# The start of a hybrid attention and mLSTM layer: its conditioned input tiles made in another order, in pairs, with the gate rows in four column groups

## The chip, the cores and the metric

The kernel runs on one core of a Trainium2 chip. The metric is the device time of one execution in microseconds (us), over 3 runs. All data are float32; inputs and outputs lie in the chip's main memory (HBM).

## What is computed

One layer of a decoder: 1024 tokens, width 1024, all parameters float32. Cut to what matters:

```python
shift, scale, gate = jnp.split(jax.nn.silu(c) @ w_ada + b_ada, 3, axis=-1)
h = x * (1.0 + scale[:, None, :]) + shift[:, None, :]
proj = h @ w_in + b_in        # 1024 x 6664: q,k,v,z | q,k,v,o,z,i,f | merge gates
y_sb = stick_breaking_attention(sb_q, sb_k, sb_v)              # 8 heads of 64
y_sb = (y_sb * silu(sb_z)) @ w_sb_proj
mq, mk = split(silu(causal_depthwise_conv(concat(ml_q, ml_k), conv_w, conv_b)))
hm = mlstm_chunkwise(mq, mk, ml_v, ml_i, log_sigmoid(ml_f))     # 4 heads of 128
y_ml = (head_norm(hm) * sigmoid(ml_o) * silu(ml_z)) @ w_ml_proj
y = (sigmoid(g_sb) * y_sb + sigmoid(g_ml) * y_ml) @ w_out
return layer_norm(alpha * x + (1.0 + gate[:, None, :]) * y, ln_g, ln_b)
```

The change concerns the first two lines and the first columns of the third.

## The kernel before

**Tiles.** The input h is kept transposed: 8 tiles `hH[:, d]` and `hL[:, d]` of 128 features by 1024 tokens. Each number is split into a high part in the rounded type fp32r and the rest, so that a product takes three matmuls: high by high, low by high, high by low (`split_product`). After the input tiles come the projection jobs (`project`, 48 matmuls of 512 tokens each), then four iterations of attention and mLSTM with further projection jobs between, the merge and the output product.

**The tile stage.** The change is in the stage that makes the 8 tiles. For each tile d:
- SyncE's queue (`block.sync`) loads 128 columns of x (`x_rows`, 512 KB) and the shift and scale columns of the conditioning weights (`a_raw`, two transfers of 512 KB). Rows of these transfers are 128 numbers, 512 B. `a_raw` has three buffers.
- VectorE (`ada_rows`) multiplies the 8 row blocks of `a_raw` by silu(c) and sums them into two accumulators, then adds these.
- TensorE (`ada_columns`) sums over partitions with a column of ones; VectorE (`mod_columns`) adds the bias and writes the shift and scale of the tile to `mod`.
- TensorE (`turn_x`) transposes x in 8 blocks of 128 x 128; ScalarE (`shifted`) applies scale and shift out of two PSUM banks into `h_raw`, and rounds it into `hH`; VectorE (`low_h`) makes `hL`.
- TensorE (`tile_of`) multiplies the tile by the first three weight chunks (`w_proH`, `w_proL`): n = 0 are the 8 columns of the input and forget gates (rows i and f), n = 1 and 2 are the first q and k. That is 18 matmuls, all with 512 tokens. Sums stay in six PSUM banks over all tiles.

Each engine works through its program in the order in which it is written, with semaphores between engines; nothing is scheduled by a planner. In the code `t.matmul(out, a, b)` holds a (the weights) still and streams b.

**What comes after.** The gate rows are copied with their bias into `r_if` (ScalarE, `bias_copy`), spread by 8 small transfers to `r_f` and `r_i` (`q` runs over four partition groups), and go through logarithms and scans on ScalarE and VectorE (`row_logs`, `row_columns`). TensorE does the jobs 3 and 4 (`project`) meanwhile, and then turns the rows into columns (`gate_columns`). The split of weight chunk 9, which the second half of job 4's columns need, stands behind `row_logs` on VectorE (`pro_split(PRO_CHUNKS + 3)`).

**The small parameters.** Seven transfers (c, the biases, the convolution weights and the norm weights) fill `prm` from SyncE's queue ahead of all else. TensorE turns `prm` into columns (`cols`), from which silu(c) is made.

## Time and profile before

| | us |
|---|---|
| median of 3 runs | 959.51 (959.13 to 959.73) |
| the profiled execution's own time | 959.67 |
| its span, first to last instruction | 957.8 |
| TensorE busy | 928.8 (97%) |
| VectorE busy | 616.0 (64%) |
| ScalarE busy | 441.2 (46%) |

All times are those of one profiled execution. PE is TensorE's matmul side, DVE VectorE, ACT ScalarE, POOL GpSimd, SP SyncE; a q behind a name is its queue, which issues transfers. Busy time of PE counts each matmul to its modelled end, so two neighbours overlap; its pace is read from start to start.

### The profile page before, as it was taken

What the parts mean: (1) busy time and instruction counts of PE and PEld (TensorE: products, weight loads), DVE (VectorE), ACT (ScalarE), POOL (GpSimd) and SP (SyncE); (2) the same over time, 40 slices, a digit from 0 to 9 for tenths busy, and PEclk for the clock granted to TensorE, in tenths of its full rate; (3) what the DMA queues carried; (4) which work ended last, traced back from release to release, by engine and by line L of the source; (5) the groups of instructions that cost most, each with busy time, mean ns of one, the idle gap of its engine ahead of it and who ended that gap; (6) DMA issues with size and microseconds to landing.
All of it is one profiled execution on the core that took longest, in us unless ns stands there. A gap on an engine that the chain in (4) does not pass through costs nothing.

```text
span 957.8 us, 12945 instructions
## 1 busy us (share of the span) xinstructions
PE 928.8 (97%) x4989; PEld 760.7 (79%) x4989; DVE 616.0 (64%) x1104; ACT 441.2 (46%) x719; POOL 165.5 (17%) x114
## 2 busy tenths in 40 slices
PE   1999999999999999999999999999999999999996
PEld 1677888888888888888888888888888888887885
DVE  4856886755976647966649867534653333345997
ACT  2454566653675544675445666525743222243100
POOL 1010132220232220322311322201100000002210
PEclk9999999999999999999999999999999999999998
DMA  8942211112201022111112111127612212215232
GB/s 221 291 110 49 66 44 34 34 35 66 78 23 45 23 55 83 40 45 34 34 44 89 43 34 34 35 55 240 211 45 66 54 45 55 88 44 186 89 132 88
DMA packets 99561, 73.96 MB, mean 77 GB/s; under 512 B 4616, under 2 KB 90760, under 8 KB 99500
## 3 DMA queue, kind: packets, MB, share of 16 engines
q1 hardware_dynamic: 94828, 58.44, 23.0%
q0 software_dynamic: 2368, 8.41, 2.7%
q10 hardware_dynamic: 2304, 6.29, 1.7%
q8 instruction: 40, 0.66, 0.3%
q14 instruction: 21, 0.17, 0.1%
HBM read 64.59 MB, written 8.40 MB: 76 GB/s over the span
## 4 chain that ended last, share of the span: by engine, by line
PE 92%; DMA 3%; DVE 2%; SPq 2%; issue 0%; ACT 0%; DVEq 0%; ACTq 0%
PE bank L643 49%; PE bank L621 9%; PE bank L622 9%; PE bank L623 9%; PE bank L762 4%; PE bank L750 3%; DMA a_raw<-in_w_ada 2%; PE bank L737 2%; PE bank L720 2%; PE bank L739 1%; PE bank L738 1%; SPq L461 1%; PE bank L785 1%; DVE a_acc L1355 1%; PE bank L787 1%; PE bank L774 1%
## 5 line engine op out<-in xcount | busy, mean ns | idle before, releaser
L643 PE MATMUL bank<-hH,wH 128*128 128x512 f32 x688 | 271.3, 394 | 0.6 <-DVE wL L1364 0.6
L643 PE MATMUL bank<-hL,wH 128*128 128x512 f32 x688 | 271.2, 394 | 0.0
L643 PE MATMUL bank<-hH,wL 128*128 128x512 f32 x688 | 271.1, 394 | 0.0
L581 POOL TENSOR_TENSOR ez<-ez,rem 128x512 f32<-128x512 f32 x72 | 134.4, 1879 | 394.3 <-DVE rem L1524 394.3
L1364 DVE SCALAR_TENSOR_TENSOR wL<-w_raw,wH 128x512 fp32r<-128x512 f32 x116 | 99.3, 860 | 108.9 <-ACT wH L938 107.8
L643 PEld LDWEIGHTS bank<-hH,wH 128*128 128x128 f32 x688 | 129.3, 188 | 30.1 <-DVE wL L1364 2.1
L643 PEld LDWEIGHTS bank<-hH,wL 128*128 128x128 f32 x688 | 129.3, 188 | 28.7 <-issue 2.9
L643 PEld LDWEIGHTS bank<-hL,wH 128*128 128x128 f32 x688 | 129.3, 188 | 28.5 <-issue 2.9
L938 ACT ACTIVATE wH<-w_raw 128x512 fp32r<-128x512 f32 x116 | 72.5, 627 | 104.4 <-PE bank L623 71.3
L1524 DVE TENSOR_TENSOR_SCAN rem<-rem,ones 128x512 f32<-128x512 f32 (+2 forms) x96 | 99.9, 1093 | 31.7 <-ACT rem L1038 31.7
L1026 ACT ACTIVATE ez<-bank 128x512 f32<-128x512 f32 x72 | 39.1, 597 | 100.6 <-PE bank L739 100.6
L623 PE MATMUL bank<-hH,wL 128*128 128x512 f32 (+1 forms) x152 | 57.6, 379 | 0.0
L622 PE MATMUL bank<-hL,wH 128*128 128x512 f32 (+1 forms) x152 | 57.6, 379 | 0.0
L621 PE MATMUL bank<-hH,wH 128*128 128x512 f32 (+1 forms) x152 | 57.5, 378 | 0.0
L610 POOL TENSOR_TENSOR yL<-yT,yH 128x1024 fp32r<-128x1024 f32 x4 | 9.7, 2424 | 210.6 <-ACT yH L1290 210.6
L1034 ACT ACTIVATE rem<-ez 128x512 f32<-128x512 f32 x72 | 41.4, 625 | 7.7 <-DVE y_stage L1531 6.1
L1038 ACT ACTIVATE rem<-rem 128x512 f32<-128x512 f32 x72 | 41.1, 621 | 0.0
L1045 ACT ACTIVATE at<-bank 128x512 f32<-128x512 f32 x72 | 38.8, 592 | 3.2 <-PE bank L750 3.2
L621 PE MATMUL bank<-hH,yH 128*128 128x512 f32 x96 | 38.1, 396 | 0.1
L622 PE MATMUL bank<-hL,yH 128*128 128x512 f32 x96 | 38.0, 396 | 0.0
L623 PE MATMUL bank<-hH,yL 128*128 128x512 f32 x96 | 37.8, 394 | 0.0
L750 PEld LDWEIGHTS bank<-ident,ez 128*128 128x128 f32 x288 | 33.5, 140 | 4.7
(247 smaller groups left out, 1508.2 us busy)
## 6 DMA issues: line engine op xcount, KB each, us to landing
w_raw<-in_w_in SPq DMA_DIRECT2D x104, 256.0 KB, 2.9
a_raw<-in_w_ada SPq DMA_DIRECT2D x16, 512.0 KB, 7.3
x_rows<-in_x SPq DMA_DIRECT2D x8, 512.0 KB, 6.4
raw<-in_w_ada POOLq DMA_DIRECT2D x8, 512.0 KB, 4.7
x_in<-in_x SPq DMA_DIRECT2D x8, 512.0 KB, 4.3
out_y<-res SPq DMA_DIRECT2D x7, 512.0 KB, 2.9
raw<-in_w_out SPq DMA_DIRECT2D x10, 256.0 KB, 4.1
m_w<-bm_scratch ACTq DMA_DIRECT2D x4, 512.0 KB, 3.7
```

The source lines that it names most:

```text
L581: g.tensor_tensor(e, e, r, ALU.mult).then_inc(a_done[h], 1)
L621: t.matmul(ps, aH, bH, start=k == 0, stop=False)
L622: t.matmul(ps, aH, bL, start=False, stop=False)
L623: return t.matmul(ps, aL, bH, start=False, stop=k == kt - 1)
L643: ins = t.matmul(banks(number)[half][:], w, a, start=(r == 0), stop=(r == JOB_MM // 2 - 1))
L750: ins = t.transpose(z_ps[h][:, b * P:(b + 1) * P], ez[s % 2][h][:, b * P:(b + 1) * P], ident[:])
L938: a.activation(wH[:, slot, :, 0:width], w_raw[:, slot, :, 0:width], ACT.Copy, scale=scale)\
L1026: a.activation(ez[s % 2][h][:], z_ps[h][:], ACT.Exp).then_inc(ex_done[h], 1)
L1034: a.activation(rem[s % 2][h][:], ez[s % 2][h][:], ACT.Ln, bias=1.0).then_inc(ln_done[h], 1)
L1038: a.activation(r, r, ACT.Exp, scale=-1.0).then_inc(rem_done[h], 1)
L1364: v.scalar_tensor_tensor(out=wL[:, slot, :, 0:width], in0=w_raw[:, slot, :, 0:width], scalar=scale, in1=wH[:, slot, :, 0:width], op0=ALU.m ...
L1524: v.tensor_tensor_scan(back, back, ones[:, 0:1].to_broadcast((P, hi - lo)), first, ALU.mult, ALU.min).then_inc(scan_done[h], 1)
```

## The change

- The transfers for c and the conditioning bias stay first on SyncE's queue. The other five parameter transfers are issued by ScalarE, and their columns are made by a second transposition.
- The conditioning weights of a tile are loaded ahead of its x, no longer behind it. Tiles 0 and 1 are handled one by one, tiles 2 to 7 in three pairs: rows of 256 numbers (1 KB), operations on 512 columns instead of 256. A pair's conditioning weights come in two pieces of 1 MB, of four row blocks each. There are four buffers instead of three; the fourth lies in the memory of `next_v` and `next_g` (now `next_vg`).
- The gate rows are no longer made from `hH` and `hL` with six matmuls a tile. `gate_rows` multiplies plain float32 rows `h_raw` of two tiles by plain float32 weights `w_if`: four matmuls, for two tiles and two halves, each with its own group of 32 output partitions of one bank. At the end VectorE adds the two tiles' sums (`if_moved`).
- `h_raw` is read by TensorE now, so `shifted` waits for `if_used`.
- The copies to `r_f` stay on SyncE's queue, those to `r_i` go to GpSimd's.
- VectorE's work is written out in an order by hand, with `low_h` between the halves of `ada_rows`.

Where a line only changes a name or a number of a semaphore it is left out here.

```diff
-A_BUFS = 3
+A_BUFS = 4
+BLOCKS = [[0], [1], [2, 3], [4, 5], [6, 7]]
+BLOCK_OF = [b for b, tiles in enumerate(BLOCKS) for _ in tiles]
 Y_BUFS = 4
 
+
+
+def pro_slot(g):
+
+    return (g // PRO_K) * (PRO_K - 1) + g % PRO_K - 1
+
+
+def ada_pieces(b):
+
+    if b < 2:
+        return [(b, 0, KT)]
+    return [(2 * b - 2 + part, part * KT // 2, (part + 1) * KT // 2) for part in range(2)]
+
+
+def ada_freed(number):
+
+    return [KT * b + hi for b in range(len(BLOCKS)) for n, _, hi in ada_pieces(b) if n == number - A_BUFS][0]
...
+        a_raw = [pt(f"a_raw{n}", [P, KT * 2 * P]) for n in range(A_BUFS - 1)] + [next_vg]
+        a_acc = pt("a_acc", [P, 2, 2, 2, 2 * P])
...
-        pro_ps = [[y_ps[0:2 * NH, :], misc_ps[2][0:2 * NH, :]],
+        pro_ps = [[y_ps[32 * n:32 * n + 2 * NH, :] for n in range(4)],
...
-            for d in range(KT):
-                cols_d = slice(d * P, (d + 1) * P)
-                sp.dma_start(x_rows[:, :, cols_d], x_v[:, :, cols_d]).then_inc(x_cols_in[d], 16)
-                if d >= A_BUFS:
-                    sp.wait_ge(ada_used, KT * (d - A_BUFS + 1))
-                for what in range(2):
-                    sp.dma_start(a_raw[:, d % A_BUFS, :, what], w_ada_w[:, :, what, cols_d])\
-                        .then_inc(a_in[d % A_BUFS], 16)
-                if d == 0:
-                    for g in range(3):
-                        pro_load(g)
-                elif d < 4:
-                    pro_load(d + 2)
+            for b, tiles in enumerate(BLOCKS):
+                cols_b = slice(tiles[0] * P, (tiles[-1] + 1) * P)
+                for number, lo, hi in ada_pieces(b):
+                    if number >= A_BUFS:
+                        sp.wait_ge(ada_used, ada_freed(number))
+                    for what in range(2):
+                        sp.dma_start(ada_piece(number, lo, hi)[:, :, what], w_ada_w[:, lo:hi, what, cols_b])\
+                            .then_inc(a_in[number % A_BUFS], 16)
+                sp.dma_start(x_rows[:, :, cols_b], x_v[:, :, cols_b]).then_inc(x_cols_in[b], 16)
+                for g in {0: range(3), 3: range(3, PRO_CHUNKS)}.get(b, ()):
+                    pro_load(g)
             for g in range(PRO_CHUNKS, 2 * PRO_JOBS):
                 pro_load(g)
             sp.wait_ge(rows_zero, 5)
-            for half in range(2):
-                sp.wait_ge(drained[half], 1)
+            sp.wait_ge(drained[1], 1)
+            sp.wait_ge(if_moved, 3)
             for q in range(4):
                 sp.dma_start(r_f[32 * q:32 * q + NH, :], r_if[NH:2 * NH, :]).then_inc(rows_in, 16)
-            for q in range(4):
-                sp.dma_start(r_i[32 * q:32 * q + NH, :], r_if[0:NH, :]).then_inc(rows_in, 16)
...
+            pool.wait_ge(drained[1], 1)
+            pool.wait_ge(if_moved, 3)
+            for q in range(4):
+                pool.dma_start(r_i[32 * q:32 * q + NH, :], r_if[0:NH, :]).then_inc(rows_i_in, 16)
...
+            def gate_rows(d):
+
+
+                for n in range(2):
+                    pe.wait_ge(m_drained[n], d + 3 - n)
+                if d % 4 == 0:
+                    pe.wait_ge(wL_done, PRO_K * (d // 4) + 1)
+                for odd in range(2):
+                    for half in range(2):
+                        ins = t.matmul(pro_ps[0][2 * odd + half], w_if[:, d + odd], h_raw[:, odd, halves(half)],
+                                       start=d == 0, stop=d == KT - 2, skip_group_check=True)
+                        if d == KT - 2 and odd:
+                            ins.then_inc(filled[half], 1)
+                if d < KT - 2:
+                    ins.then_inc(if_used, 1)
...
+            turn_x(0)
             ada_columns(0)
-            for d in range(KT):
-                turn_x(d)
-                if d:
-                    tile_of(d - 1, 0, PRO_K - 1)
-                if d + 1 < KT:
-                    ada_columns(d + 1)
-                if d:
-                    tile_of(d - 1, PRO_K - 1, PRO_K)
-            tile_of(KT - 1, 0, PRO_K)
+            turn_x(1)
+            for d in range(0, KT, 2):
+                tile_of(d, 1)
+                if d == 0:
+                    ada_columns(1)
+                tile_of(d, 2)
+                gate_rows(d)
+                if d + 2 < KT:
+                    if d:
+                        ada_columns(BLOCK_OF[d + 2])
+                    turn_x(d + 2)
+                    if not d:
+                        ada_columns(BLOCK_OF[d + 2])
+                tile_of(d + 1, 1)
+                tile_of(d + 1, 2)
+                if d + 3 < KT:
+                    turn_x(d + 3)
...
+            for row, src in [(ROW_B, bi[0:OFF_IF]), (ROW_GSB, bi[OFF_GSB:OFF_GSB + 2 * D]), (ROW_CB, conv_b[0]),
+                             (ROW_NG, ml_norm_g[0])]:
+                src = src.rearrange("(t p) -> t p", p=P)
+                act.dma_start(prm[row:row + src.shape[0], :], src).then_inc(params_in, 16)
...
+                act.wait_ge(mod_done, BLOCK_OF[d] + 1)
                 if d > 1:
+                    act.wait_ge(if_used, d // 2)
...
+            def ada_rows(b, lo, hi):
+
+                if lo == 0 and b > 1:
+                    dve.wait_ge(ada_done, b - 1)
+                for k in range(lo, hi):
+                    for number, first, _ in ada_pieces(b):
+                        if k == first:
+                            dve.wait_ge(a_in[number % A_BUFS], 32 * (number // A_BUFS + 1))
+                    acc, row = ada_sum(b, k % 2), ada_row(b, k)
                     if k < 2:
                         v.tensor_scalar(acc, row, silu_c[:, k:k + 1], None, ALU.mult).then_inc(ada_used, 1)
                     else:
-                        dve.wait_ge(ada_used, KT * d + k - 1)
+                        dve.wait_ge(ada_used, KT * b + k - 1)
                         v.scalar_tensor_tensor(out=acc, in0=row, scalar=silu_c[:, k:k + 1], in1=acc,
                                                op0=ALU.mult, op1=ALU.add).then_inc(ada_used, 1)
-                dve.wait_ge(ada_used, KT * (d + 1))
-                v.tensor_tensor(a_acc[:, d % 2, 0], a_acc[:, d % 2, 0], a_acc[:, d % 2, 1], ALU.add)\
-                    .then_inc(ada_summed, 1)
...
+            other_columns()
+            ada_rows(0, 0, KT)
+            mod_columns(0)
+            for g in range(3):
+                pro_split(g)
+            ada_rows(1, 0, KT // 2)
+            low_h(0)
+            ada_rows(1, KT // 2, KT)
+            ada_rows(2, 0, KT // 4)
+            mod_columns(1)
+            ada_rows(2, KT // 4, KT)
+            low_h(1)
+            mod_columns(2)
+            ada_rows(3, 0, KT // 2)
+            low_h(2)
+            ada_rows(3, KT // 2, KT)
+            low_h(3)
+            for g in range(3, PRO_CHUNKS):
+                pro_split(g)
+            mod_columns(3)
+            ada_rows(4, 0, KT // 2)
+            low_h(4)
+            ada_rows(4, KT // 2, KT)
+            low_h(5)
+            mod_columns(4)
+            low_h(6)
+            low_h(7)
             for g in range(PRO_CHUNKS, PRO_CHUNKS + 3):
                 pro_split(g)
+            dve.wait_ge(filled[1], 1)
+            dve.wait_ge(rows_zero, 5)
+            rows = [r_if[0:2 * NH, halves(half)] for half in range(2)]
+            v.tensor_copy(rows[1], pro_ps[0][1]).then_inc(if_moved, 1)
+            dve.wait_ge(if_moved, 1)
+            v.tensor_tensor(rows[1], pro_ps[0][3], rows[1], ALU.add).then_inc(if_moved, 1)
+            dve.wait_ge(drained[0], 1)
+            v.tensor_tensor(rows[0], pro_ps[0][2], rows[0], ALU.add).then_inc(if_moved, 1)
```

VectorE, before: its work for tile 6 and the start of tile 7. A row is line, operation, output<-inputs, shape, and the semaphores that it waits for.

```order
L1352 TENSOR_SCALAR a_acc<-a_raw,silu_c 128x256 [waits ada_done,ada_in0]
L1352 TENSOR_SCALAR a_acc<-a_raw,silu_c 128x256
L1355 SCALAR_TENSOR_TENSOR a_acc<-a_raw,silu_c,a_acc 128x256 [waits ada_used] x6
L1358 TENSOR_TENSOR a_acc<-a_acc 128x256 [waits ada_used]
L1381 TENSOR_TENSOR hL<-h_raw,hH 128x1024 [waits hH_done]
L1387 TENSOR_TENSOR mod<-bank,cols 128x1 [waits ada_done]
L1388 SCALAR_TENSOR_TENSOR mod<-bank,cols 128x1
L1352 TENSOR_SCALAR a_acc<-a_raw,silu_c 128x256 [waits ada_done,ada_in1]
```

VectorE, after: its work for the last pair, tiles 6 and 7, with the low parts of tiles 4 to 7 (`hL`).

```order
L1431 TENSOR_SCALAR a_acc<-a_raw,silu_c 128x512 [waits ada_in2,ada_done]
L1431 TENSOR_SCALAR a_acc<-a_raw,silu_c 128x512
L1434 SCALAR_TENSOR_TENSOR a_acc<-a_raw,silu_c,a_acc 128x512 [waits ada_used] x2
L1462 TENSOR_TENSOR hL<-h_raw,hH 128x1024 [waits hH_done]
L1434 SCALAR_TENSOR_TENSOR a_acc<-next_vg,silu_c,a_acc 128x512 [waits ada_used,ada_in3]
L1434 SCALAR_TENSOR_TENSOR a_acc<-next_vg,silu_c,a_acc 128x512 [waits ada_used] x3
L1438 TENSOR_TENSOR a_acc<-a_acc 128x512 [waits ada_used]
L1462 TENSOR_TENSOR hL<-h_raw,hH 128x1024 [waits hH_done]
L1468 TENSOR_TENSOR mod<-bank,cols 128x2x2 [waits ada_done]
L1462 TENSOR_TENSOR hL<-h_raw,hH 128x1024 [waits hH_done] x2
```

One operation now covers two tiles; the shift and scale of tiles 6 and 7 appear together, after the second piece of weights, and both low parts come behind them.

TensorE, before: the end of tile 7 in front of the first projection job, from the gate rows on.

```order
L621 MATMUL bank<-hH,w_proH 8x512 [waits hL_done]
L622 MATMUL bank<-hL,w_proH 8x512
L623 MATMUL bank<-hH,w_proL 8x512
L621 MATMUL bank<-hH,w_proH 8x512
L622 MATMUL bank<-hL,w_proH 8x512
L623 MATMUL bank<-hH,w_proL 8x512
L621 MATMUL bank<-hH,w_proH 128x512
L622 MATMUL bank<-hL,w_proH 128x512
L623 MATMUL bank<-hH,w_proL 128x512
```

TensorE, after: the end of tile 6, the gate rows of tiles 6 and 7, and the start of tile 7.

```order
L647 MATMUL bank<-hH,w_proH 128x512
L648 MATMUL bank<-hL,w_proH 128x512
L649 MATMUL bank<-hH,w_proL 128x512
L716 MATMUL bank<-h_raw,w_if 8x512 [waits misc_drained1,misc_drained0]
L716 MATMUL bank<-h_raw,w_if 8x512 x3
L647 MATMUL bank<-hH,w_proH 128x512 [waits hL_done]
L648 MATMUL bank<-hL,w_proH 128x512
L649 MATMUL bank<-hH,w_proL 128x512
```

The six matmuls per tile with 8 weight columns are gone; four per pair stand in the middle of the pair.

SyncE's queue, before: what stands behind the tile stage's loads.

```order
L447 DMA w_raw<-in_w_in 128x4x128 [waits wL_done] x4
L474 DMA r_f<-r_if 4x1024 [waits proj_drained1,proj_drained0,rows_zero]
L474 DMA r_f<-r_if 4x1024 x3
L476 DMA r_i<-r_if 4x1024 x4
L447 DMA w_raw<-in_w_in 128x4x128 [waits wL_done] x82
```

SyncE's queue, after: the last pair's loads and the same place.

```order
L486 DMA a_raw<-in_w_ada 128x4x256 [waits ada_used]
L486 DMA a_raw<-in_w_ada 128x4x256
L486 DMA next_vg<-in_w_ada 128x4x256 [waits ada_used]
L486 DMA next_vg<-in_w_ada 128x4x256
L488 DMA x_rows<-in_x 128x8x256
L472 DMA w_raw<-in_w_in 128x4x128 [waits wL_done] x4
L497 DMA r_f<-r_if 4x1024 [waits if_moved,proj_drained1,rows_zero]
L497 DMA r_f<-r_if 4x1024 x3
L472 DMA w_raw<-in_w_in 128x4x128 [waits wL_done] x82
```

The copies to `r_f` wait for VectorE's additions (`if_moved`), and the four copies to `r_i` have left this queue.

## Rows read from the trace of the kernel before

**Rows 1.** The page: each engine's busy time, share and instructions

```profile
PE 928.8 (97%) x4989; PEld 760.7 (79%) x4989; DVE 616.0 (64%) x1104; ACT 441.2 (46%) x719; POOL 165.5 (17%) x114
```

**Rows 2.** PE's waits from 0 to 110 us: us in total, times, longest

```profile
PE bank L659 <- DVE a_acc L1358: 15.1, 4, 10.1
PE bank L643 <- DVE wL L1364: 0.6, 1, 0.6
```

**Rows 3.** Stretches: busy PE, PEld, DVE, ACT, POOL, clock, DMA share, GB/s

```profile
15.00:20.00 5.00, 2.96 (x12) 2.50 (x12) 2.76 (x10) 1.93 (x3) 0.00 (x0) 1.00 0.99 226
30.00:55.00 25.00, 23.82 (x126) 17.25 (x126) 20.22 (x52) 10.56 (x13) 0.00 (x0) 1.00 1.20 290
657.00:660.00 3.00, 3.00 (x15) 2.48 (x14) 1.15 (x1) 2.01 (x2) 0.00 (x0) 1.00 1.01 407
```

**Rows 4.** SyncE's queue in order of time: start, us, what is issued

```profile
1.62 0.76 SPq L438 DMA_DIRECT2D prm<-in_b_in  x2
3.47 0.43 SPq L457 DMA_DIRECT2D x_rows<-in_x  x1
68.19 2.55 SPq L474 DMA_DIRECT2D r_f<-r_if  x4
70.79 2.44 SPq L476 DMA_DIRECT2D r_i<-r_if  x4
```

**Rows 5.** DVE in order of time: start, us, operation (its idle time before)

```profile
11.85 0.62 DVE L1352 TENSOR_SCALAR a_acc<-a_raw,silu_c 128x256 f32<-128x256 f32 x2 [4.85 <-DMA a_raw<-in_w_ada]
55.09 0.62 DVE L1352 TENSOR_SCALAR a_acc<-a_raw,silu_c 128x256 f32<-128x256 f32 x2 [0.56 <-DMA a_raw<-in_w_ada]
64.12 1.23 DVE L1381 TENSOR_TENSOR hL<-h_raw,hH 128x1024 fp32r<-128x1024 f32 x1 [4.15 <-ACT hH L966]
65.26 1.89 DVE L1364 SCALAR_TENSOR_TENSOR wL<-w_raw,wH 128x512 fp32r<-128x512 f32 x3
77.15 0.69 DVE L1409 TENSOR_SCALAR r_e<-r_e 128x1024 f32<-128x1024 f32 x1 [10.00 <-ACT r_e L1013]
83.64 0.69 DVE L1364 SCALAR_TENSOR_TENSOR wL<-w_raw,wH 128x512 fp32r<-128x512 f32 x1
101.98 0.54 DVE L1574 TENSOR_SCALAR m_k<-conv_in,h_col 128x512 f32<-128x512 f32 x1
102.56 1.54 DVE L1576 SCALAR_TENSOR_TENSOR m_k<-conv_in,h_col,m_k 128x512 f32<-128x512 f32 x2
```

**Rows 6.** PE in order of time, in the tile stage and behind it

```profile
24.00 1.94 PE L671 MATMUL bank<-ident,x_rows 128*128 128x128 f32 x8 [0.41 <-DVE mod L1388]
58.92 0.50 PE L659 MATMUL bank<-ones,a_acc 128*128 128x1 f32 x4
60.76 1.04 PE L671 MATMUL bank<-ident,x_rows 128*128 128x128 f32 x8
69.79 0.39 PE L623 MATMUL bank<-hH,w_proL 128*128 128x512 f32 x1
70.02 0.39 PE L643 MATMUL bank<-hH,wH 128*128 128x512 f32 x1
```

**Rows 7.** ACT in order of time

```profile
61.48 1.45 ACT L962 ACTIVATE h_raw<-bank,mod 128x512 f32<-128x512 f32 x2 [2.90 <-PE bank L671]
63.02 1.06 ACT L966 ACTIVATE hH<-h_raw 128x1024 fp32r<-128x1024 f32 x1
74.96 1.06 ACT L1011 ACTIVATE r_e<-r_f 128x1024 f32<-128x1024 f32 x1 [4.06 <-DMA r_i<-r_if]
```

**Rows 8.** PE in order of time: plain float32 matmuls of 128 columns

```profile
151.83 0.39 PE L785 MATMUL bank<-m_vtok,m_ktok 128*128 128x129 f32 x2
152.05 0.39 PE L787 MATMUL bank<-m_state,m_q 128*128 128x129 f32 x2
152.37 1.97 PE L762 MATMUL bank<-at,v_tok 128*64 128x128 f32 x32
```

**Rows 9.** A transfer by GpSimd's queue: count, KB, us from issue to landing

```profile
r_bias<-in_b_in POOLq DMA_DIRECT2D x1, 0.0 KB, 5.1
```

More of the change, by code:

```diff
@@ L1009, in _ @@
                 if n == 2:
-                    act.wait_ge(rows_in, 16 * 8)
+                    act.wait_ge(rows_in, 16 * 4)
                     a.activation(r_e[:], r_f[:], ACT.Exp, scale=-1.0).then_inc(f_ln, 1)
@@ L1391, in _, with mod_columns @@
[L1391 to L1401 removed]
+            def mod_columns(b):
+                dve.wait_ge(ada_done, b + 1)
+                first, tiles = BLOCKS[b][0], len(BLOCKS[b])
+                bias = cols[:, ROW_ADA:ROW_ADA + 2 * KT].rearrange("p (w d) -> p w d", w=2)[:, :, first:first + tiles]
+                v.tensor_tensor(mod[:, :, first:first + tiles],
+                                ada_ps[:, 0:2 * tiles].rearrange("p (w d) -> p w d", w=2), bias, ALU.add)\
+                    .then_inc(mod_done, 1)
```

162 lines of the change are left out of this document (83 added, 79 removed).

## The prediction

> **What bounds the kernel now.** The page first: PE is busy for 97% of the span [rows 1], so time can only be won where PE waits or where it does more work than needed. The waits of PE between 0 and 110 us come next: 15.1 us behind the sums of the conditioning weights, the longest 10.1, and 0.6 us behind a weight split in the first projection jobs [rows 2]. So the loss lies at the start. The stretches then say what feeds those sums: from 30 to 55 us the transfer engines move 290 GB/s at a share over 1, and PE is busy for 23.82 of 25 us [rows 3]. Both run at one pace. A tile needs 1.57 MB, which is 5.4 us at 291 GB/s; its PE work is 18 matmuls at 0.233 us (start to start, 69.79 to 70.02), eight transposes (about 0.87 by their starts) and the column sums, again 5.4 us [rows 6]. The first weights arrive at 11.85 and the last at 55.09 [rows 5]. PE's last tile ends at 70.02, where job 3 begins [rows 6]. A gain in this stage needs an earlier start, and both paces shorter.
>
> **Start of the loads.** In the trace x is issued at 3.47 [rows 4], and x and weights of tile 0 (1.57 MB, 5.4 us) are there at 11.85 [rows 5]: landing = issue + 3.0 + bytes / rate. The same rule for tile 7 (13.66 MB with weight chunks) gives 3.5 + 3.0 + 46.9 = 53.4 against 55.09; 1.1 of the rest is the dip to 226 GB/s between 15 and 20 us, where the queue waited for a split [rows 3], so 0.6 is drift. Five of the seven parameter transfers leave this queue, so the first weights are issued in the slot of 1.62 [rows 4]: base 4.6. Being ahead of x they land at 4.6 + 3.6 = 8.2. silu(c) needs only the two transfers that stay first, and the other columns are made while the weights fly; ScalarE has nothing else to do at that time. I cost these at nothing; if they came late, they would show up to about 1 us.
>
> **Pace of the loads.** Rows of 1 KB do not occur in the trace. Bounds: 291 GB/s, as 512 B rows, and 407, as between 657 and 660 us, when rows of 4 KB are loaded [rows 3]. A packet costs each of the 16 engines 28.2 ns at 512 B and 161 ns at 4 KB; the straight line between gives 47.1 ns at 1 KB, that is 348 GB/s, which I take. A pair (3.15 MB) needs 9.0 us then (10.8 and 7.7 by the bounds). The Trainium skill speaks against this gain: in "DMA: Bandwidth & Descriptors", Specifications, 512 B is already enough for line rate. By it the pairs would stay at 291; 291 against 407 in this trace speaks for some cost per row, but no row tests 1 KB.
>
> **Pace of PE.** The gate rows cost six matmuls a tile, 2.8 us a pair. In their place stand four plain float32 ones. The trace has such matmuls of 128 columns: 0.22 us for one (two instructions, starts 151.83 and 152.05), so 0.88 for 512 columns. Sixteen with 64 output partitions, alternating between two column groups, take 1.97 us, 0.12 each: side by side [rows 8]. Bounds for the four: 0.88 us, if all four groups run together, and 3.5, if none do; two at a time 1.9. I take 0.95, since the rows show groups overlapping nearly fully. A pair costs PE 24 x 0.233 + 0.95 + 1.8 + 0.4 = 8.7 us, after 10.9.
>
> **Pace of VectorE.** 512-column operations: 0.54 for a scaled copy, 0.77 for multiply-add [rows 5], so a pair's sum is 2 x 0.54 + 6 x 0.77 + 0.7 = 6.4, plus two low parts at 1.2: 8.8 us. It has no slack either, and its order is fixed, so I follow the chain.
>
> **The chain to the end of the stage.** The piece with the first half of the last pair's weights has before it 3.69 MB at 291 (12.7 us), two pairs of 6.29 MB at 348 (18.1) and 0.54 MB of chunks (1.9), and takes 3.0 itself: 4.6 + 35.7 + 0.4 drift = 40.7. Then, on VectorE: 2.6 for its four row blocks, 1.2 for the low part of tile 4, 3.8 for the other four blocks and the addition: 48.3. PE's column sums 0.5 (0.50 in [rows 6]), beside the low part of tile 5 (1.2), then the bias: 49.5. ScalarE applies and rounds tile 6 in 2.6 (61.48 to 64.1 in [rows 7]): 52.1. Low part 1.2: 53.3. PE: tile 6 2.8, gate rows 0.95, tile 7 2.8: 59.9. PE's own queue fits under it: from tile 4 at 44.5, tiles, gate rows, sums and transposes up to tile 6 are 8.7 us. The other load, tile 7's rounding, is done during tile 6.
>
> PE's first work runs at its lower level: eight transposes took 1.94 us at 24.0, after PE had waited, and 1.04 at 60.76, 1.2 against 2.4 GHz, though the granted clock reads 1.00 in both stretches [rows 3, 6]. The changed stage has gaps of about 2 us until 26. If the level rises at 30 the delay left at the end is 0.5: 60.4. **The stage ends 9.6 us sooner than 70.02.**
>
> **Behind the stage.** Job 3 follows without a pause, its chunks are split by then. The next wait is chunk 9's split behind the row chain. Its start: gate rows end at 57.6; but VectorE has the low part of tile 7 and three splits (1.9, [rows 5]) ahead, until 59.3, and then the new copy and two additions on 8 rows of 512, 2.0: 61.3, against 68.19 for the first copy to `r_f` [rows 4], 6.9 sooner. The four copies to `r_i` no longer stand between (2.44, [rows 4]), and ScalarE's first row operation waited for the last of them, at 74.96 [rows 7]. So the chain is 9.3 sooner, and PE's wait grows from 0.6 to 0.9. Copies to `r_i`: four issues take about 2.4 to 2.5, as on SyncE's queue [rows 4], and one transfer by GpSimd landed after 5.1 at most [rows 9]: 61.3 + 2.4 + 5.1 = 68.8; VectorE wants them at 77.15 - 9.3 = 67.9, so 0.9 at worst, nothing at the 1.8 or so that the copies on SyncE's queue took (issued until 73.2, used at 74.96). Queued behind GpSimd's wait is only work of the first iteration.
>
> **Sum.** 9.6 - 0.3 = 9.3. Against the profiled execution's own 959.67, with a span of 957.8: 950.4; the median of the runs is 0.2 lower: **950.2 us**. Everything behind is tied to PE's order and shifts as a whole.
>
> **The rivals.**
> - *Transfers stay at 291.* The 7.34 MB of the pairs up to the piece take 25.2 instead of 21.1: 954.3. For it: no row has 1 KB, and the rate held at 290 for 25 us, a steady limit. Against it: 407 with longer rows. The Trainium skill's rule on 512 B, above, would give this time. Chance 0.14.
> - *The gate rows run one after another.* 3.5 per pair. PE's pair is 11.3 then, more than the loads', and the end comes 5.6 later (2.55 in the last pair, the rest carried from the one before, less the slack there): 955.8. Against it: the pairs in [rows 8]. Two at a time: about 951.8. Chance 0.12.
> - *PE's lower level again, for part of the stage.* PE's work from tile 0's first matmul at 18.9 is 34.5 us at the upper level (22.4 + 3.8 + 6.3 transposes + 2.0). Low until 40, the end is 40 + 34.5 - 10.5 = 64.0: 953.8. Chance 0.09.
> - *The same to the end: slower.* The sum reaches 70.0 if the level is low beyond 52 us; low throughout it is 18.9 + 69 = 88, so 18 us slower than before, 977. For it: the level was low at 24 us, after waits, and the changed stage waits for loads again and again. Against it: gaps from 30 us on are 2 us at most, by the schedule above, while the low transposes at 24 came after waits up to 10.1 [rows 2]. The Trainium skill, "TensorE: Matmul & The Clock Gate", section "What's actually happening", has activity release the throttle and idling restore it. The trace agrees, with 1.94 and 1.04 us. Chance 0.05.
> - *The row chain takes the place of the loads.* If `r_i` is at its worst: 0.9 more, 951.3. Chance 0.04.
> - *It does not do what it says:* had the row chain kept its place in time, for a reason that I don't see, PE would wait for it and get nothing: 959.5. Chance 0.04.
> - The forecast itself: 0.52.
>
> **How the numbers follow.** The range's lower end is the 4 KB rate for pairs (2.1 us sooner at the end, where VectorE takes over), no cost of the lower level (0.5) and 0.6 for the waits that I rounded up: 947.0. Its upper end holds the sequential gate rows: 956.0. Outside lie the slower case, no change, and two of the costs together, under 2 in 10. A change under 0.2%, 1.9 us, could not be told from none. Faster by more: 0.52 + 0.14 + 0.12 + 0.09 + 0.04, less a little, is 0.90; the same 0.04; slower 0.06.
>
> **What would show it.** The first operation on weights at about 8.2; a load rate near 348 GB/s between 20 and 45 us; eight gate instructions of a pair within about 1 us; the first projection job at about 60.4; a wait of 0.9 us before chunk 9's use. It is wrong if the transposes between 30 and 60 us take 1.9 us, if the rate reads 291, or if PE waits at the transposition of the rows.

## The result, and the profile after

The changed kernel takes 954.41 us, the median of four runs (953.26 to 955.91), against 959.45 (959.13 to 959.73) for the kernel before in the same series: a ratio of 0.9949, 95% interval 0.9937 to 0.9960. It is faster by 5 us, and the time lies inside the range of 947.0 to 956.0; the forecast itself, 950.2, was 4.2 too low. The profiled execution is the slowest of the four (955.91, span 953.3 against 957.8 before). It is 3.8 us below the profiled execution before (959.67) and its span 4.5 below that one's, since time and span lie 2.6 apart here and 1.9 before; what fills that difference, no row shows. Its rows are read first; a second profile of the same kernel stands with the experiments, and the two differ in a way that matters.

The page of the changed kernel, engine-busy row as in [rows 1]:

```profile
PE 925.0 (97%) x4974; PEld 757.7 (79%) x4974; DVE 613.6 (64%) x1069; ACT 440.6 (46%) x719; POOL 167.7 (18%) x118
```

PE's waits from 0 to 105 us after the change, the view of [rows 2]:

```profile
PE bank L703 <- DMA x_rows<-in_x: 7.6, 3, 4.2
...
PE bank L647 <- DVE hL L1462: 3.0, 2, 2.7
...
PE bank L669 <- DVE wL L1443: 1.8, 1, 1.8
PE bank L669 <- ACT next_q L1047: 1.3, 1, 1.3
```

The 15.1 us behind the sums of the weights are gone. L703 is the transposition of x (L671 before), L647 a tile's first product, L669 the projection jobs. Two waits stand behind the tile stage now, where before there was one of 0.6: 1.8 for chunk 9's split, and 1.3 at the start of job 3, which the prediction does not have.

VectorE in order of time, the first operation on the weights of tiles 0, 1 and of the three pairs (the first piece of each), as in [rows 5]:

```profile
8.34 0.61 DVE L1431 TENSOR_SCALAR a_acc<-a_raw,silu_c 128x256 f32<-128x256 f32 x2
...
15.26 0.61 DVE L1431 TENSOR_SCALAR a_acc<-a_raw,silu_c 128x256 f32<-128x256 f32 x2 [0.95 <-DMA a_raw<-in_w_ada]
...
20.13 0.88 DVE L1431 TENSOR_SCALAR a_acc<-a_raw,silu_c 128x512 f32<-128x512 f32 x2 [0.29 <-DMA a_raw<-in_w_ada]
...
29.16 0.88 DVE L1431 TENSOR_SCALAR a_acc<-a_raw,silu_c 128x512 f32<-128x512 f32 x2 [0.73 <-DMA a_raw<-in_w_ada]
...
41.47 0.88 DVE L1431 TENSOR_SCALAR a_acc<-a_raw,silu_c 128x512 f32<-128x512 f32 x2 [2.02 <-DMA a_raw<-in_w_ada]
...
47.50 0.69 DVE L1438 TENSOR_TENSOR a_acc<-a_acc 128x512 f32<-128x512 f32 x1
```

All but the first of the five wait for their load, so these starts are the landings. The first stands right behind the other columns (until 8.31); its own load had landed by 7.7 (issued at 2.1, 5.6 to landing). Now stretches of the same kernel, the view of [rows 3] (busy time of PE, PEld, DVE, ACT, POOL, granted clock, DMA share, GB/s):

```profile
20.00:45.00 25.00, 20.78 (x115) 15.25 (x115) 19.81 (x32) 13.92 (x18) 0.00 (x0) 1.00 1.11 341
45.00:50.00 5.00, 5.00 (x20) 2.90 (x20) 4.29 (x6) 0.00 (x0) 0.00 (x0) 0.66 0.69 177
50.00:55.00 5.00, 5.00 (x34) 4.05 (x30) 0.50 (x2) 2.51 (x3) 0.00 (x0) 1.00 0.00 0
```

The loads run at 341 GB/s over those 25 us: 347, 349 and 347 in the five-us stretches of pairs alone (from 20, 25 and 40 us), 327 and 333 between 30 and 40 us, after three chunk loads with their rows of 512 B were issued from 26.36 on. The straight line between two packet costs held. The middle row is new: a granted clock of 0.66, and only 20 instructions in five full us. PE in order of time shows where it comes from, the view of [rows 6]:

```profile
41.16 1.03 PE L703 MATMUL bank<-ident,x_rows 128*128 128x128 f32 x8
44.87 0.50 PE L647 MATMUL bank<-hH,w_proH 128*128 128x512 f32 x1 [2.67 <-DVE hL L1462]
...
46.14 0.47 PE L649 MATMUL bank<-hH,w_proL 128*128 128x512 f32 x1
46.41 0.63 PE L647 MATMUL bank<-hH,w_proH 128*128 128x512 f32 x1
46.84 0.63 PE L648 MATMUL bank<-hL,w_proH 128*128 128x512 f32 x1
...
49.10 1.33 PE L716 MATMUL bank<-h_raw,w_if 128*8 128x512 f32 x8
50.36 1.05 PE L692 MATMUL bank<-ones,a_acc 128*128 128x1 f32 x8
...
58.95 1.04 PE L716 MATMUL bank<-h_raw,w_if 128*8 128x512 f32 x8
...
64.28 0.47 PE L669 MATMUL bank<-hH,wH 128*128 128x512 f32 x1 [1.28 <-ACT next_q L1047]
```

After a pause of 2.67 us the products of tile 4 first start 0.23 us apart, and from 46.41 on 0.43 apart: PE's lower level. It is back at the upper one for the column sums (L692), which start at 50.36, though VectorE had their inputs by 48.2. From tile 4's start to those sums it is 5.49 us. Gate rows (L716, eight instructions for the four matmuls of a pair) take 1.33 where the level rises again among them and 1.04 at the upper level throughout; from 58.95 to the next tile at 59.92 it is 0.97. The last row is the missing "without a pause": job 3 waits 1.28 us for ScalarE.

ScalarE in order of time at that place, as in [rows 7], with SyncE's and GpSimd's copies of the gate rows, as in [rows 4], below it:

```profile
60.13 0.68 ACT L1047 ACTIVATE r_if<-bank,r_bias 8x512 f32<-8x512 f32 x1 [0.27 <-PE bank L716]
62.84 0.72 ACT L1047 ACTIVATE r_if<-r_if,r_bias 8x512 f32<-8x512 f32 x1 [2.03 <-DVE r_if L1506]
63.47 1.23 ACT L1047 ACTIVATE next_q<-bank,cols 128x512 f32<-128x512 f32 x2
...
70.46 1.06 ACT L1081 ACTIVATE r_e<-r_f 128x1024 f32<-128x1024 f32 x1 [4.62 <-DMA r_f<-r_if]
```

```profile
63.64 2.57 SPq L497 DMA_DIRECT2D r_f<-r_if  x4
```

```profile
64.12 2.07 POOL L597 DMA_DIRECT2D r_i<-r_if  x4 [4.15 <-ACT r_if L1047]
```

ScalarE takes its work in program order: the second half of the gate rows waits 2.03 us for VectorE's addition, and the copy of `next_q`, which empties the banks that job 3 wants, stands behind it. The row chain then starts at 70.46, against 74.96 before: 4.5 sooner, not 9.3.

### The profile page after: what moved, and what is told of

Read it like the earlier page. It is cut to its first block, busy times and chain, and to the rows that moved or that the text cites. A ratio compares the mean times of both kernels' runs of the same rounds, so it can differ in the third digit from the quotient of the medians.

```text
span 953.3 us, 12891 instructions
## 1 busy us (share of the span) xinstructions
PE 925.0 (97%) x4974; PEld 757.7 (79%) x4974; DVE 613.6 (64%) x1069; ACT 440.6 (46%) x719; POOL 167.7 (18%) x118
## 4 chain that ended last, share of the span: by engine, by line
PE 92%; DMA 3%; DVE 3%; SPq 1%; ACT 1%; issue 0%; DVEq 0%; ACTq 0%
PE bank L669 49%; PE bank L647 9%; PE bank L649 9%; PE bank L648 9%; PE bank L818 4%; PE bank L806 3%; DMA a_raw<-in_w_ada 2%; PE bank L793 2%; PE bank L776 2%; PE bank L795 1%; PE bank L794 1%; PE bank L841 1%; PE bank L843 1%; PE bank L830 1%; PE bank L838 1%; DVE a_acc L1434 1%
## 5 line engine op out<-in xcount | busy, mean ns | idle before, releaser
L669 PE MATMUL bank<-hH,wH 128*128 128x512 f32 x688 | 271.2, 394 | 3.0 <-DVE wL L1443 1.8
L669 PE MATMUL bank<-hL,wH 128*128 128x512 f32 x688 | 271.1, 394 | 0.0
L669 PE MATMUL bank<-hH,wL 128*128 128x512 f32 x688 | 270.9, 394 | 0.0
L669 PEld LDWEIGHTS bank<-hH,wH 128*128 128x128 f32 x688 | 129.3, 188 | 32.9 <-issue 3.7
L669 PEld LDWEIGHTS bank<-hH,wL 128*128 128x128 f32 x688 | 129.2, 188 | 28.8 <-issue 2.9
L669 PEld LDWEIGHTS bank<-hL,wH 128*128 128x128 f32 x688 | 129.2, 188 | 28.5 <-issue 2.9
L647 PE MATMUL bank<-hH,wH 128*128 128x512 f32 (+1 forms) x152 | 57.5, 378 | 0.0
L647 PE MATMUL bank<-hH,yH 128*128 128x512 f32 x96 | 38.0, 395 | 0.1
```

Of the source, the lines that this page charges most:

```text
L647: t.matmul(ps, aH, bH, start=k == 0, stop=False)
L669: ins = t.matmul(banks(number)[half][:], w, a, start=(r == 0), stop=(r == JOB_MM // 2 - 1))
```

## The experiments

Theory 1: the pause before tile 4 lets PE's level fall. Theory 2: VectorE's additions stand too late, and ScalarE's queue passes that on to job 3. Theory 3: the copies to `r_f` are slow because something runs beside them, by 3a the weight loads issued right behind, by 3b the copies to `r_i` on GpSimd's queue. Theory 4: the landing of the last pair's first weights sets the end of the stage. Theory 5: PE's own work counts only in the last two pairs. Each run was timed beside the kernel before, whose medians were 959.82, 959.46 and 959.49 in the three series. The changed kernel's own 954.41 and 952.68 (below) are the references; its nine runs lie between 952.64 and 955.91, so a difference of medians under about 1.5 us decides nothing here by itself, and the rows have to.

**Unused matmuls in the pause.** Twenty of 256 columns ahead of tile 4, into a bank that nobody reads then.

```diff
+                if d == 4:
+                    for _ in range(20):
+                        t.matmul(misc_ps[2][:, HALF // 2:HALF], w_proH[:, 0, 0], hH[:, 0, 0:HALF // 2],
+                                 start=True, stop=True)
                 tile_of(d, 1)
```

> The changed kernel with 20 matmuls of 256 columns (about 2.3 us) put in TensorE's pause before tile 4; they write to an unused part of a PSUM bank and nobody reads them. Theory 1: in the changed kernel TensorE fell to its lower level at 46.3 us, after its pause from 42.2 to 44.9, and that made the stage 2 to 2.5 us longer; with the pause filled the matmuls of tile 4 start 0.23 us apart throughout, the column sums of the last pair start near 48.3 instead of 50.4, job 3 starts near 62.0 instead of 64.3 and the time is about 952. Rival: the chain of loads and VectorE sets the end anyway; the level does not matter and the time stays at 954 to 955.

Measured 953.36 (952.98 to 953.74, five runs), ratio 0.9933 [0.9919, 0.9947], span 951.7. Its stretches on PE (busy time, clock, DMA share, GB/s) and PE in order of time:

```profile
45.00:50.00 5.00, 5.00 (x32) 1.00 0.67 170
```

```profile
48.90 1.05 PE L692 MATMUL bank<-ones,a_acc 128*128 128x1 f32 x8
...
62.82 0.47 PE L669 MATMUL bank<-hH,wH 128*128 128x512 f32 x1 [1.28 <-ACT next_q L1051]
```

In tile 4 the level stays up (1.00, 32 instructions for 20), the column sums start 1.46 us sooner and job 3 with them. The median is 1.1 below 954.41, half of what was expected, and 0.7 above 952.68; neither decides anything. More telling is the spread: 0.8 us where the changed kernel has 2.65.

**The additions ahead of the splits** on VectorE.

```diff
-            for g in range(PRO_CHUNKS, PRO_CHUNKS + 3):
-                pro_split(g)
             dve.wait_ge(filled[1], 1)
...
             v.tensor_tensor(rows[0], pro_ps[0][2], rows[0], ALU.add).then_inc(if_moved, 1)
+            for g in range(PRO_CHUNKS, PRO_CHUNKS + 3):
+                pro_split(g)
```

> The changed kernel with VectorE's three copy-and-add operations on the gate rows ahead of its three weight splits instead of behind them. Theory 2: job 3 waits 1.3 us for ScalarE's copy of the first q, which stands behind the gate rows' second half, which waits for VectorE; with the additions 1.9 us earlier that wait goes, the row chain starts 1.5 to 1.9 sooner (first copy to r_f near 61.9 instead of 63.6), the wait for chunk 9 (1.8) shrinks only by what job 3 does not gain, and the time is 1.3 to 1.9 lower, about 952.8. Rival: the splits themselves are then late for job 3 (first one needed at 62.8), the wait changes its name and the time stays.

Measured 955.16 (953.95 to 956.94, five runs), 0.9953 [0.9940, 0.9965], span 953.5. ScalarE, then SyncE's queue:

```profile
60.88 0.72 ACT L1047 ACTIVATE r_if<-r_if,r_bias 8x512 f32<-8x512 f32 x1 [0.72 <-DVE r_if L1504]
...
69.04 1.06 ACT L1081 ACTIVATE r_e<-r_f 128x1024 f32<-128x1024 f32 x1 [5.16 <-DMA r_f<-r_if]
```

```profile
62.19 0.37 SPq L472 DMA_DIRECT2D w_raw<-in_w_in  x1
62.68 2.64 SPq L497 DMA_DIRECT2D r_f<-r_if  x4
```

Theory 2 is right about the place: job 3 starts at 62.32 with no wait. But the row chain is only 1.4 sooner, and 0.65 of that is there already at the column sums (49.71 for 50.36). Ahead of the copies to `r_f` SyncE's queue holds a weight load that waits for the first of the splits, and these now come later: the copies are issued 1.1 behind the end of ScalarE's work on the gate rows, in the changed kernel 0.1. So chunk 9's wait grows from 1.8 to 2.3, and part of the removed wait is handed on. PE behind that wait, and the stretch:

```profile
78.47 0.50 PE L669 MATMUL bank<-hH,wH 128*128 128x512 f32 x1 [2.31 <-DVE wL L1443]
...
80.02 0.63 PE L669 MATMUL bank<-hH,wH 128*128 128x512 f32 x1
80.45 0.63 PE L669 MATMUL bank<-hL,wH 128*128 128x512 f32 x1
```

```profile
80.00:85.00 5.00, 5.00 (x17) 0.67 0.15 45
```

Here the level falls a second time. Chunk 9's first product is 1.4 sooner than in the changed kernel (78.47 for 79.89), but from there to the end of the span it takes 875.0 us, where both profiles of the changed kernel take 873.4. The fall behind the longer wait took back, in this execution, what the edit had won.

**The copies apart.** First SyncE holds its next loads until the copies to `r_f` have landed; then, in another kernel, GpSimd holds the copies to `r_i` so long, and VectorE waits for those only in front of the scan that reads them.

```diff
                 sp.dma_start(r_f[32 * q:32 * q + NH, :], r_if[NH:2 * NH, :]).then_inc(rows_in, 16)
+            sp.wait_ge(rows_in, 16 * 4)
```

> The changed kernel with SyncE waiting until the four r_f copies have landed before it issues the next weight loads. Theory 3: the copies landed 4 us after their last issue (1.7 expected) because two 256 KB loads are issued directly behind them on the same queue; without these ScalarE's first row operation starts near 67.9 instead of 70.5, the wait of 1.8 us for chunk 9 goes and the time is 1.5 to 1.8 lower, about 952.7. Rival 3b: the copies to r_i on GpSimd's queue, at the same time from the same memory, hold them up; then ScalarE still starts at 70.0 to 70.5 and the time stays at 954.4.

```diff
             pool.wait_ge(if_moved, 3)
+            pool.wait_ge(rows_in, 16 * 4)
...
-                dve.wait_ge(rows_i_in, 16 * 4)
                 link(v.tensor_scalar(r_e[:], r_e[:], -1.0, -SOFT_CAP, ALU.mult, ALU.max))
...
+                dve.wait_ge(rows_i_in, 16 * 4)
                 link(v.tensor_tensor_scan(r_m[:], r_f[:], r_i[:], 0.0, ALU.add, ALU.max))
```

> The changed kernel with GpSimd's copies to r_i issued only once r_f has landed; VectorE waits for r_i only before the scan that reads it, 4.2 us later than before. Theory 3 (the weight loads behind hold r_f up): ScalarE's first row operation stays near 70.5, and the time at 954.4. Rival 3b (the r_i copies hold r_f up): it starts near 68 and the time is 1.5 to 1.8 lower, about 952.7.

Loads held: 952.64 (952.20 to 954.95, five runs), 0.9933 [0.9920, 0.9945], span 952.4. `r_i` held: 951.82 (950.89 to 953.05, four runs), 0.9919 [0.9905, 0.9932], span 950.9. ScalarE, from the second half of the gate rows to the first row operation, loads held and then `r_i` held:

```profile
62.61 0.72 ACT L1048 ACTIVATE r_if<-r_if,r_bias 8x512 f32<-8x512 f32 x1 [2.03 <-DVE r_if L1507]
...
69.55 1.06 ACT L1082 ACTIVATE r_e<-r_f 128x1024 f32<-128x1024 f32 x1 [3.94 <-DMA r_f<-r_if]
```

```profile
62.45 0.72 ACT L1048 ACTIVATE r_if<-r_if,r_bias 8x512 f32<-8x512 f32 x1 [2.04 <-DVE r_if L1507]
...
67.52 1.06 ACT L1082 ACTIVATE r_e<-r_f 128x1024 f32<-128x1024 f32 x1 [2.06 <-DMA r_f<-r_if]
```

From row to row that is 7.62 us in the changed kernel (62.84 to 70.46; 7.39 to 7.55 in six more profiles with this order), 6.94 without the loads and 5.07 without the `r_i` copies. So 3b carries 2.3 to 2.5 us and 3a 0.5 to 0.7. In the medians, `r_i` held is 2.6 and 0.9 below the two references, loads held 1.8 and nothing. With `r_i` held, chunk 9's wait is gone. The two sets of copies stand on two queues and run together; side by side, the set that is wanted first is late.

**Pairs loaded in rows of 512 B**, everything else as in the changed kernel.

```diff
-                        sp.dma_start(ada_piece(number, lo, hi)[:, :, what], w_ada_w[:, lo:hi, what, cols_b])\
...
+                        for n, d in enumerate(tiles):
+                            sp.dma_start(ada_piece(number, lo, hi)[:, :, what, n * P:(n + 1) * P],
+                                         w_ada_w[:, lo:hi, what, d * P:(d + 1) * P])\
```

> The changed kernel with the pairs' loads cut into transfers of 128 columns (rows of 512 B, as before); order, buffers and all operations stay. Theory 4 (the loads set the start of the last pair, and 1 KB rows bring 348 instead of 290 GB/s): the rate is 290 GB/s again, the first operation of the last pair starts 4 us later than 41.5, and the time is 4 higher, about 958.4. Rival: VectorE's and TensorE's chain has slack of its own; the time is less than 1.5 higher.

Measured 959.50 (958.63 to 960.49, eleven runs), 1.0002 [0.9993, 1.0010], span 958.0: the whole gain is gone. Its stretches on PE and VectorE's first operation on the last pair:

```profile
20.00:45.00 25.00, 22.25 (x115) 0.93 1.21 288
50.00:55.00 5.00, 5.00 (x18) 0.59 0.76 195
```

```profile
45.33 0.88 DVE L1436 TENSOR_SCALAR a_acc<-a_raw,silu_c 128x512 f32<-128x512 f32 x2 [2.36 <-DMA a_raw<-in_w_ada]
```

288 GB/s after 341, and the last pair lands 3.9 us later (45.33 after 41.47; 4.6 after the second profile's 40.77). The time lost is 5.1 to 6.8 against the two medians. Beside the second profile the column sums are 7.0 later: 4.6 by the landing, and 2.4 since tile 4 takes 6.39 us to them in place of 3.97, with the clock at 0.59 in 50 to 55 us after a wait of 3.6. The Trainium skill, "DMA: Bandwidth & Descriptors", Specifications, has 512 B already at line rate; this pair of runs, alike but for the row length, measures 288 and 341, so here the measurement decides against it.

**x ahead of the weights**, the order of before, in each block of tiles.

```diff
+                sp.dma_start(x_rows[:, :, cols_b], x_v[:, :, cols_b]).then_inc(x_cols_in[b], 16)
                 for number, lo, hi in ada_pieces(b):
...
-                sp.dma_start(x_rows[:, :, cols_b], x_v[:, :, cols_b]).then_inc(x_cols_in[b], 16)
```

> The changed kernel with x ahead of the conditioning weights in every block, as before. Theory 4: what counts is when the last pair's first weights arrive; 1 MB of x ahead of them costs 3.0 us at 348 GB/s, the first operation of the last pair starts near 44.5, and the time is 3 higher, about 957.4. Rival: TensorE waited 7.6 us for x in the changed kernel; with x earlier the tiles 0 to 3 come earlier, and the time is at most 1 higher.

Measured 956.85 (955.92 to 958.08, seven runs), 0.9972 [0.9961, 0.9983], span 954.2. The pairs' first operations are at 23.35, 32.37 and 43.84 where they were at 20.13, 29.16 and 41.47. That is 2.4 to 3.2 us later, and the time is 2.4 to 4.2 longer: what lands first is worth its bytes. The rival, at most 1 higher, fell.

**Each gate matmul twice** (the gate sums are doubled, so the output is not the reference's).

```diff
-                for odd in range(2):
-                    for half in range(2):
...
+                for odd, half, again in [(o, h, r) for r in range(2) for o in range(2) for h in range(2)]:
...
```

> The changed kernel with each gate matmul done twice (8 instead of 4 a pair, 0.98 us more of TensorE per pair; the sums of the gate rows are doubled, so the output is not the reference's). Theory 5: TensorE's own time counts only in the last two pairs, so 1.5 to 2.0 us come in, about 956.2; then the six matmuls a tile of the kernel before (1.8 us a pair more than now) would cost about 3. Rival: every pair counts, 3.9 more, 958.3; or the chain of VectorE and ScalarE hides all but the last pair, 1.0 more, 955.4.

Measured 954.01 (953.87 to 954.12, five runs), 0.9944 [0.9930, 0.9957], span 952.1. PE in order of time:

```profile
44.50 0.50 PE L647 MATMUL bank<-hH,w_proH 128*128 128x512 f32 x1 [1.54 <-DVE hL L1461]
...
47.51 1.90 PE L715 MATMUL bank<-h_raw,w_if 128*8 128x512 f32 x16
49.34 1.05 PE L692 MATMUL bank<-ones,a_acc 128*128 128x1 f32 x8
```

Sixteen instructions take 1.90, so four more matmuls cost 0.9, and the four column groups do run together. Job 3 starts at 63.27, 1.2 behind the second profile of the changed kernel: 0.9 by the gate rows of tiles 4 and 5 and 0.3 by a later landing. The doubled rows of the last pair cost nothing, since PE's wait for ScalarE shrinks from 1.3 to 0.4. Theory 5 asked for 1.5 to 2.0; one pair counted, not two. The spread is 0.25 us, the smallest of all, and the clock is 1.00 in every stretch of five us from 20 to 75; the pause before tile 4 is 1.54.

**The changed kernel once more**, in that series.

> The changed kernel as it is, beside the three others. All theories: 953.3 to 956, median 954.4, with more spread than the kernel before, since TensorE's level falls at a slightly different place in each run (theory 1).

Measured 952.68 (952.64 to 954.71, five runs), 0.9935 [0.9923, 0.9948], span 950.9. Stretches on PE and PE in order of time:

```profile
25.00:30.00 5.00, 4.17 (x22) 0.82 1.10 349
30.00:35.00 5.00, 5.00 (x23) 0.83 1.14 327
45.00:50.00 5.00, 5.00 (x35) 1.00 0.68 172
```

```profile
44.16 0.50 PE L647 MATMUL bank<-hH,w_proH 128*128 128x512 f32 x1 [1.48 <-DVE hL L1462]
48.13 1.05 PE L692 MATMUL bank<-ones,a_acc 128*128 128x1 f32 x8
...
62.06 0.47 PE L669 MATMUL bank<-hH,wH 128*128 128x512 f32 x1 [1.29 <-ACT next_q L1047]
```

The same program, and here the pause is 1.48 and the level stays in tile 4. Job 3 starts 2.2 us sooner than in the first profile. Tile 4 itself starts 0.7 sooner (44.16 for 44.87), as the weights land 0.7 sooner; the other 1.5 is the price of the fallen level, 5.49 from tile 4 to the column sums after 3.97. The same three steps hold in the other profiles without unused matmuls: 3.4 us from the landing of the last pair's first weights to tile 4, 3.97 to 3.99 on to the sums where the level stays behind a pause of 1.45 or 1.48, 5.46 to 5.53 where it falls (6.39 with the narrow rows), and 13.92 to 13.93 on to job 3 wherever that waits for ScalarE.

The level fell here too, but earlier: from 28.50 to 31.06 the products of tile 1 start 0.43 apart. That cost nothing, for PE had to wait for tile 4 in any case; it only made the pause shorter. The unused matmuls above, whose job 3 started at 62.82, are 0.8 behind this execution, and 0.6 of that is there at the landing (41.37 for 40.77). The wait of 1.29 for ScalarE is there in both, so it belongs to the kernel; the level belongs to the execution.

**The five parameter transfers back on SyncE's queue**, ahead of the weights.

```diff
+            for row, src in [(ROW_B, bi[0:OFF_IF]), (ROW_GSB, bi[OFF_GSB:OFF_GSB + 2 * D]), (ROW_CB, conv_b[0]),
+                             (ROW_NG, ml_norm_g[0])]:
...
+                sp.dma_start(prm[row:row + src.shape[0], :], src).then_inc(params_in, 16)
...
```

> The changed kernel with the five other parameter transfers on SyncE's queue again, behind c and the bias and ahead of the first weights. Theory 4: all loads shift by their 1.85 us (1.62 to 3.47), the first operation of the last pair starts near 43 and the time is 1.85 higher than the changed kernel's beside it in the earlier call (952.7), about 954.5. Rival: the five transfers are tiny, the loads catch up behind them, and the time is within 0.5 of the changed kernel's.

Measured 955.27 (954.53 to 957.43, five runs), 0.9957 [0.9943, 0.9970], span 954.8. The first operations are at 9.32, 16.93, 21.79, 30.83 and 43.21, about 1.7 us later than in the changed kernel's first profile from the second on. For the first it is 1.0, because that one now waits for its load and did not there. The medians differ by 0.9 and 2.6, so it is the rows that say that the loads do not catch up. In this profile, too, the clock falls (0.78 between 45 and 50 us), and it is the longest run of its kernel.

**The two mended together** (additions first, `r_i` held), **and with fourteen unused matmuls** in the pause. The diffs are those above.

> The additions ahead of the splits and the late r_i copies together, no filler. With the row chain 2.5 us quicker, the 1.3 us wait of job 3 is no longer handed on to chunk 9: 951.8 (late r_i copies alone) less 1.3, about 950.5, with a spread of 2 to 3 us by where TensorE's level falls. If job 3's wait was worth nothing by itself: 951.8.

> The same with 14 filler matmuls (1.6 us) in the pause before tile 4. Theory 1: the level never falls in tile 4, the spread is under 1 us and the median is 0.5 to 1 lower than without, about 949.8. Rival: the filler delays tile 4 by as much as it saves, and both medians agree within 0.5.

Without the unused matmuls 951.88 (950.19 to 953.41, five runs), 0.9920 [0.9908, 0.9933], span 950.1; with them 950.69 (950.09 to 951.09, four runs), 0.9909 [0.9895, 0.9922], span 949.2. The second one's stretches on PE, ScalarE, and PE's wait behind the stage:

```profile
45.00:50.00 5.00, 5.00 (x32) 1.00 0.66 172
```

```profile
60.04 0.72 ACT L1052 ACTIVATE r_if<-r_if,r_bias 8x512 f32<-8x512 f32 x1 [0.72 <-DVE r_if L1509]
...
66.40 1.06 ACT L1086 ACTIVATE r_e<-r_f 128x1024 f32<-128x1024 f32 x1 [3.36 <-DMA r_f<-r_if]
```

```profile
PE bank L670 <- DVE wL L1448: 0.5, 1, 0.5
```

Job 3 starts at 61.47 without a wait. This is the lowest median of the study, 3.7 us below the changed kernel's first and 2.0 below its second, and within 0.5 of the forecast, which the changed kernel itself did not reach. That the three mends add up isn't shown by the medians: the combination without fill (951.88) is no lower than `r_i` held alone (951.82), though its profile loses only 0.3 before chunk 9 and nothing before job 3, and fill against no fill is 1.2 with ranges that overlap. In its profile PE came to the pause at 43.27, 0.8 before tile 4 could begin (3.4 behind the landing at 40.63), and the fill held tile 4 until 45.00, 1.0 late: here the fill cost more than it could save. The combination without fill has runs at 950.19 and 950.94 too, with a mean clock of 0.997, and at 951.88 to 953.41 with 0.994.

## Why the prediction was right, and where it was not

- **Start of the loads**: 8.2 predicted for the landing, 7.7 measured. The agreement of 8.34 with 8.2 is luck: VectorE began 0.6 after the landing, held by the other columns, which were "cost at nothing". It did no harm, as tile 1's weights were waited for again at 15.26. Putting the parameters back made landings about 1.7 late, and x first made them 2.4 to 3.2 late.
- **Pace of the loads**: 348 predicted, 347 to 349 measured, and the first piece of the last pair at 41.47 and 40.77 for 40.7. With rows of 512 B the whole gain is gone: the landings alone carry about 4 of those 5 to 7 us. The rival of 291 GB/s fell.
- **Gate rows**: 0.95 a pair predicted, 0.97 by starts. The rival of one after another fell with the doubled matmuls, 0.9 for four.
- **VectorE's pace** was costed too high: 0.44 a scaled copy and 0.68 a multiply-add of 512 columns (0.88 and 2.73 over 2 and 4), for 0.54 and 0.77. So its second four row blocks did not set the column sums, as the prediction has it: VectorE is done 0.6 before them in the second profile and 2.2 in the first (47.5 for 48.13, 48.2 for 50.36), and what they wait for is tile 4, ahead of them on PE.
- **The chain to the stage's end**: 60.4 predicted. In the second profile PE could begin job 3 at 60.77 (62.06 less its wait), in the first only at 63.00. The step that failed in the first is "the delay left at the end is 0.5", the price of PE's lower level: I let it rise once at 30 and stay. It rose at about 22 us, and of that early stretch nothing is left, since PE pauses before tile 4 in both profiles; it fell again behind a pause of 2.67 us and cost 1.5 us there. The other 0.7 is the later landing of the weights. That the second profile comes so near to 60.4 is in part luck: the 0.5 that wasn't due stands against a way from the sums to the stage's end of 12.6 us, where 11.6 was costed. The rival "lower level again, for part of the stage" (953.8) thus came true in that execution, though at a later place and not in all; the other rival of the level, slower than before, did not.
- **"Job 3 follows without a pause"** is wrong in both profiles: 1.28 and 1.29 us. I had looked at the chunks that job 3 reads and not at the banks that it writes. They are emptied by ScalarE's copy of `next_q`, which stands in its queue behind the new addition on VectorE, which stands behind three splits. I had even placed that addition (61.3), and did not ask who waits behind ScalarE's half of the gate rows. With the additions first, the wait is gone.
- **The row chain "9.3 sooner"** is 4.5. The issue of `r_f` came at 63.64, not 61.3, most of it late with the stage's end, and then the copies landed 4.3 us behind the last issue (66.21 to 70.46) where `r_i` before took 1.73. I had charged GpSimd's copies for being late themselves; what they did was to slow the ones beside them, by 2.3 to 2.5 us. PE's wait for chunk 9 is 1.8 in place of 0.9.

The sum for the first profile: PE could begin job 3 at 63.00, 7.0 sooner than 70.02; the wait in front of it takes 1.3, the longer wait for chunk 9 1.2 (1.8 less 0.6): 4.5, which is what the spans show (957.8 less 953.3). Of the 9.3 predicted, 4.8 is missing: 1.5 went to PE's level, 0.7 to the later landing, 1.3 to ScalarE's queue, 0.9 to the copies (1.8 for 0.9), and 0.4 is the stage's end in itself (60.77 for 60.4). In the second profile the first two are absent, and the span is 6.9 below the one before.

What decides in an execution whether the pause before tile 4 is 1.5 or 2.7 us is half known. Of the 1.2 between the two profiles, 0.7 is the landing of the weights (41.47 and 40.77), and 0.5 is PE, which comes to the pause later in the second (42.68 for 42.20) by its fall at 28 us. Of the 0.7, half is there from the first issue for tile 1 on (7.61 and 7.24, first operations at 15.26 and 14.91); where the rest comes from wasn't found.

That the level makes the spread of the runs is argued, not shown. For it: the kernels with added work, whose profiles keep the level in tile 4, have spreads of 0.25, 0.8 and 1.0, after 2.65 and 2.07. Against it: with x first the profile keeps the level in tile 4 too (pause 1.45), and the spread is 2.2. The mean clocks don't decide: the longest run, 955.91, has 0.997 and a shorter one, 954.00, has 0.995, for the mean also takes in the early fall and the last microseconds of the kernel, when PE has nothing left to do (0.54 over 946 to 951 us in the second profile). And 0.8 of the 3.2 us between 955.91 and 952.68 lies outside the span (2.6 and 1.8 between time and span).

Not run back singly, and so without a share in the gain of their own: the fourth buffer, the operations on 512 columns, the order of VectorE's work, and the six matmuls a tile for the gate rows.

## What to carry to other kernels

When work is moved into an engine's queue, ask what stands behind it on every engine that waits for it, and who needs the banks that this work frees, not only whose data it makes; a wait taken away ahead of another (here job 3's ahead of chunk 9's) is in part handed on, and the longer wait can bring PE's level down, which here cost 1.6 us more. To find what a late stretch costs, look for the points that it must pass (here landing, tile 4, column sums, job 3) and compare the distances between them over several profiles: two executions of one program differed by 2.2 us at job 3 by two causes, which one pair of start times mixes. Loads at the bound of a stage are best cut to longer rows first, here 512 B to 1 KB for about 4 us. Small copies that are wanted one after the other should be issued so, even where a second queue is free.
